# Expert up product with the weights as the stationary operand, in a one-core Trainium2 kernel

## The reference

```python
def expert_block(args):
    tok, wgt, e = args
    xb = h[tok]
    hid = jax.nn.silu(xb @ exp_gate[e]) * (xb @ exp_up[e])
    return (hid @ exp_down[e]) * wgt[:, None]
```

## Time and profile before

| | |
|---|---|
| median of 3 runs | 2751.93 us (2748.4 to 2758.2) |
| profiled execution: time | 2754.09 us |
| profiled execution: span | 2751.3 us |
| TensorE busy | 2628.2 us, 96% of the span |
| VectorE busy | 1655.5 us, 60% |
| ScalarE busy | 726.8 us, 26% |
| granted TensorE clock, mean over the span | 0.978 of full speed |
| moved by DMA | 347.50 MB |

### The profile page before, as it was taken

The page is one execution under the profiler, slowest core; times in us unless marked ns, Lnnn a source line. Parts: engine busy times, 40 slices in busy tenths (PEclk is TensorE's granted clock), DMA queues, the critical chain, the costliest instruction groups (busy, mean ns, idle before and its releaser), DMA issues. The chain is left out here.

```text
span 2751.3 us, 54243 instructions
## 1 busy us (share of the span) xinstructions
PE 2628.2 (96%) x21528; PEld 1725.3 (63%) x21528; DVE 1655.5 (60%) x4435; ACT 726.8 (26%) x1772; POOL 310.8 (11%) x415
## 2 busy tenths in 40 slices
PE   6999989999999999999999999999999898899996
PEld 4888856664588744688544467777777655444443
DVE  5444267786555657665556368888888667322225
ACT  3211056651310000000000246555666300100002
POOL 0000033310000000000000000111110100634312
PEclk9999999999999999999999999999999999899998
DMA  6010035331022346223445411100000030799995
GB/s 247 32 62 31 1 138 170 124 110 45 30 78 92 138 168 214 68 86 110 152 170 180 157 63 29 29 3 29 29 21 11 18 126 31 291 397 401 399 365 206
DMA packets 108845, 347.50 MB, mean 126 GB/s; under 512 B 8752, under 2 KB 18480, under 8 KB 99520
## 3 DMA queue, kind: packets, MB, share of 16 engines
q1 hardware_dynamic: 100160, 319.00, 31.9%
q0 software_dynamic: 8448, 25.18, 2.5%
HBM read 311.05 MB, written 33.10 MB: 125 GB/s over the span
## 5 line engine op out<-in xcount | busy, mean ns | idle before, releaser
L2076 PE MATMUL mixing_ps<-all_main,pre_ws 64*64 64x256 f32 x3072 | 245.9, 380 | 0.0
L3096 PE MATMUL ex_ps<-all_main,ex_xT 128*128 128x512 f32 x512 | 231.9, 596 | 12.1 <-DVE ex_xT L3250 10.2
L1318 PE MATMUL mlp_ps<-mlp_w2s,all_main 128*128 128x512 f32 x512 | 239.6, 592 | 0.0
L1318 PE MATMUL mlp_ps<-all_main 128*128 128x512 f32 x384 | 183.2, 592 | 0.7 <-DVE all_main L1541 0.7
L3096 PEld LDWEIGHTS ex_ps<-all_main,ex_xT 128*128 128x128 f32 x512 | 95.2, 191 | 121.4 <-issue 117.6
L1318 PEld LDWEIGHTS mlp_ps<-mlp_w2s,all_main 128*128 128x128 f32 x512 | 96.6, 190 | 117.8 <-issue 105.1
L2076 PEld LDWEIGHTS mixing_ps<-all_main,pre_ws 64*64 64x64 f32 x3072 | 126.5, 134 | 27.2 <-issue 4.0
L254 PE MATMUL qkv_ps<-qkv_wq,h_hT 128*128 128x256 f32 x576 | 134.0, 385 | 2.9 <-DVE h_hT L547 2.9
L1318 PEld LDWEIGHTS mlp_ps<-all_main 128*128 128x128 f32 x384 | 72.7, 190 | 93.2 <-issue 70.2
L254 PEld LDWEIGHTS qkv_ps<-qkv_wq,h_hT 128*128 128x128 f32 x576 | 111.1, 193 | 19.7 <-issue 4.1
L1532 DVE TENSOR_TENSOR all_main<-mlp_w2s 128x512 f32<-128x512 f32 x64 | 44.2, 690 | 131.1 <-PE mlp_ps L1318 129.5
(11 more groups left out here) (486 smaller groups left out, 5041.6 us busy)
## 6 DMA issues: line engine op xcount, KB each, us to landing
mlp_w2s<-in_w SPq DMA_DIRECT2D x64, 1024.0 KB, 5.0
all_main<-in_w_gu SPq DMA_DIRECT2D x32, 2048.0 KB, 14.8
all_early<-in_w SPq DMA_DIRECT2D x32, 1024.0 KB, 4.8
att_wa<-in_w_ada SPq DMA_DIRECT2D x32, 512.0 KB, 3.9
all_early<-in_w_d SPq DMA_DIRECT2D x16, 1024.0 KB, 17.4
all_main<-in_w_d SPq DMA_DIRECT2D x16, 1024.0 KB, 17.4
y_rows<-ex_y SPq DMA_DIRECT2D x32, 512.0 KB, 9.8
qkv_wq<-in_w_qkv SPq DMA_DIRECT2D x6, 2048.0 KB, 7.5
```

What stands on the lines that cost most here:

```text
L1318: last = nc.tensor.matmul(ps[:, PRODUCTS.index(name), :], lhsT=lhsT, rhs=rhs, start=j == 0, stop=j == FPAIRS - 1)
L2076: last = nc.tensor.matmul(ps[heads(m), banks[half], 0:UT], lhsT=ws[heads(half), n, k, heads(m)], rhs=columns(k, heads(half)), start=(k == ...
L3096: last = nc.tensor.matmul(pg[:, n % 2, :], lhsT=xT[:, n % 2, k * P:(k + 1) * P], rhs=gu[n][:, k, :], start=(k == 0), stop=(k == KT - 1))
```

## The change

In the up product the operands change places. Blocks of 128 columns of `gu` (cell c of 4, slice k of 8) are stationary and the 128 gathered rows of `xT` stream. The result in `pg` has hidden features on partitions and rows along the free axis: columns 0 to 255 hold the two gate blocks, 256 to 511 the two up blocks. Silu and the multiply keep their shapes, and `hid` comes out as `hT` was. The turns, the copy to `hT`, the accumulators `ph`, the tile `hT` and the semaphores `h_turned` and `h_taken` go. The up product is 32 matmuls in place of 8, split 20 and 12 where it was 5 and 3. With no turn between them, the two parts follow one another. The waits for reuse of `hid` are now on `downed`.

```diff
-                def up(ring, b, n, ks):
-                    for k in ks:
-                        last = nc.tensor.matmul(pg[:, n % 2, :], lhsT=xT[:, n % 2, k * P:(k + 1) * P], rhs=gu[n][:, k, :], start=(k == 0),
-                                                stop=(k == KT - 1))
-                    if ks[-1] == KT - 1:
+                def up(ring, b, n, cells):
+                    for cell in cells:
+                        c, k = cell // KT, cell % KT
+                        last = nc.tensor.matmul(pg[:, n % 2, c * P:(c + 1) * P], lhsT=gu[n][:, k, c * P:(c + 1) * P],
+                                                rhs=xT[:, n % 2, k * P:(k + 1) * P], start=(k == 0), stop=(k == KT - 1))
+                    if cells[-1] == CELLS - 1:
                         last.then_inc(ring.gated, 1)
-
-                def turn_h(ring, b, n):
-                    for j in range(2):
-                        last = nc.tensor.transpose(ph[:, n % 2, j * P:(j + 1) * P], hid[:, n % 2, j * P:(j + 1) * P], ident[:])
-                    last.then_inc(ring.h_turned, 1)
 
                 def down(ring, b, n):
                     for half in range(2):
                         for j in range(2):
-                            last = nc.tensor.matmul(py[:, half, :], lhsT=hT[:, n % 2, j, :],
+                            last = nc.tensor.matmul(py[:, half, :], lhsT=hid[:, n % 2, j * P:(j + 1) * P],
                                                     rhs=dn[n][:, j, half * NB:(half + 1) * NB], start=(j == 0), stop=(j == 1))
                     last.then_inc(ring.downed, 1)
 
-                FIRST, REST = range(0, 5), range(5, KT)
+                CELLS = 4 * KT
+                FIRST, REST = range(0, 20), range(20, CELLS)
...
-                def p_turn_h(b, n):
+                def p_down(b, n):
                     pe.wait_ge(pipe.hidden, b + 3)
-                    pe.wait_ge(pipe.h_taken, b + 1)
-                    turn_h(pipe, b, n)
-
-                def p_down(b, n):
-                    pe.wait_ge(pipe.h_taken, b + 3)
                     pe.wait_ge(pipe.y_taken_a, b + 1)
                     pe.wait_ge(pipe.y_taken_v, b + 1)
                     down(pipe, b, n)
...
                         p_up_first(b + 1, (n + 1) % NW, j + 1 + (n + 1) // NW)
-                        p_turn_h(b, n)
                         up(pipe, b + 1, (n + 1) % NW, REST)
                         p_down(b, n)
...
                 def p_hidden(b, n):
                     dve.wait_ge(pipe.silu, b + 1)
-                    dve.wait_ge(pipe.h_turned, b + 1)
+                    dve.wait_ge(pipe.downed, b + 1)
                     hidden(pipe, b, n)
-
-                def p_take_h(b, n):
-                    dve.wait_ge(pipe.h_turned, b + 3)
-                    dve.wait_ge(pipe.downed, b + 1)
-                    take_h(pipe, b, n)
...
                         p_turn_x(b + 2, (n + 2) % NW, j + 1 + (n + 2) // NW)
-                        p_take_h(b, n)
                         p_hidden(b + 1, n + 1)
                         p_take_y(b, n, 2 * j + n // 2 + 1)
```

More of the change, by code:

```diff
@@ L2949, in stage_experts_combine @@
         hid = s.sb("hid", [P, 2, D_EXP])
-        hT = s.sb("hT", [P, 2, 2, P])
         y = s.sb("y", [P, 2, D])
@@ L2963, in stage_experts_combine @@
         ps = s.ps("ps", [P, 2 * RING, NB])
-        plist, pg, ph, py = (ps[:, 2 * n:2 * n + 2, :] for n in range(4))
-        names = "x_turned gated silu hidden h_turned h_taken downed y_taken_a y_taken_v"
+        plist, pg, py = (ps[:, 2 * n:2 * n + 2, :] for n in (0, 1, 3))
+        names = "x_turned gated silu hidden downed y_taken_a y_taken_v"
         class Ring:
@@ L2971, in stage_experts_combine @@
         for ring, tag in ((pipe, "p"), (more, "o")):
-            (ring.x_turned, ring.gated, ring.silu, ring.hidden, ring.h_turned, ring.h_taken, ring.downed,
+            (ring.x_turned, ring.gated, ring.silu, ring.hidden, ring.downed,
              ring.y_taken_a, ring.y_taken_v) = (s.sem(f"{tag}_{n}") for n in names.split())
@@ L3143, in _ @@
                 pe.sem_inc(pipe.gated, 2)
-                pe.sem_inc(pipe.h_turned, 2)
                 pe.sem_inc(pipe.downed, 2)
@@ L3158, in _ @@
                         p_up_first(b + 1, (b + 1) % NW, EXPERTS // NW)
-                    p_turn_h(b, b % NW)
                     if b + 1 < EXPERTS:
@@ L3180, in _ @@
                         pe.wait_ge(more.x_turned, b + 2)
-                        up(more, b, 0, range(KT))
+                        up(more, b, 0, range(CELLS))
                         pe.wait_ge(more.hidden, b + 1)
-                        turn_h(more, b, 0)
-                        pe.wait_ge(more.h_taken, b + 1)
                         down(more, b, 0)
@@ L3260, in hidden @@
                                             ).then_inc(ring.hidden, 1)
-                def take_h(ring, b, n):
-                    nc.vector.tensor_copy(hT[:, n % 2, :, :].rearrange("p a b -> p (a b)"), ph[:, n % 2, 0:2 * P]
-                                          ).then_inc(ring.h_taken, 1)
                 def take_y(ring, b, n):
@@ L3355, in _ @@
                 nc.vector.memset(eps[:], LN_EPS).then_inc(scaled, 1)
-                dve.sem_inc(pipe.h_taken, 2)
                 dve.sem_inc(pipe.y_taken_v, 1)
@@ L3371, in _ @@
                         p_turn_x(b + 2, (b + 2) % NW, EXPERTS // NW)
-                    p_take_h(b, b)
                     if b + 1 < EXPERTS:
@@ L3389, in _ @@
                         hidden(more, b, 0)
-                        dve.wait_ge(more.h_turned, b + 1)
-                        take_h(more, b, 0)
                         dve.wait_ge(more.downed, b + 2)
```

## The result

The changed kernel takes 2763.37 us (median of 9 runs, 2760.11 to 2766.67), the kernel before 2752.47 (9 runs beside them, 2747.12 to 2758.2). The ratio is 1.004 with a 95% interval of 1.003 to 1.0051: 10.9 us or 0.4% slower. The profiled execution of after has a time of 2763.37 us and a span of 2761.6, against 2751.3 before, so there are 10.3 us of span to find.

A forecast was written before the change was run, and what follows sets the result against it. TensorE, busy 96% of the span, was taken as the bound, with DMA full beside it at 400 GB/s. +1.4 - 0.3 = +1.1 us on the 2751.9 median gave 2753.0 us; own range 2749 to 2758, whole range 2745 to 2775.

The forecast's parts named there:

- The pitch: Up product: each of 64 records, a 128x128 load with 128 moving columns, takes 0.1117 us, so 7.15 us a block.
- the period: Steady expert block: 7.15 us up plus 3.43 us down is 10.58 us, +0.06 us a block.
- the 24 later blocks: Blocks 8 to 31, from 2441.43 us to the end: +0.06 us each, +1.4 us together.
- the last block: Before down(31): without turns it waits only for y's copy, so it starts 0.33 us sooner and most of 1.28 stays.
- the rate: DMA in the expert stage: a little under the earlier 400 GB/s, at 396.
- the weights' earlier landing: Gate and up weights in the expert stage: time from issue to landing falls below 14.3 us.
- slower: Whole kernel more than 0.3% (8.3 us) slower: chance 0.20.
- part 2: Turns and copy: hidden copy gains nothing; the first seven blocks' 0.4 us disappears in TensorE's 5.5 us of weight waits.
- Rival A: Every up record: weight loads don't hide; +28 us at a pitch of 0.125, +220 us with nothing hidden; chance 0.11.
- Rival C: Expert stage: DMA bounds at a 10.46 us period, waits for w_d appear, -1.7 us, 2750 us; chance 0.10.
- Rival B: TensorE's loop: larger code is fetched again at six jumps back, 10 to 31 us, 2763 to 2784 us; chance 0.15.
- the forecast's mechanism: Whole kernel: +1.4 us over the later blocks and -0.3 us before the last down product, +1.1 us.

The follow-up runs named there:

- after_spread: Changed kernel with all gathers kept but their series broken up by GpSimd's comparisons and, in the loop, a wait on an earlier up product: 2750.53 us, 0.9995 of before.
- before_split: Kernel before, operands and turns kept, with each 512 moving columns of the up product in four matmuls of 128: 2766.58 us, 1.0055.
- 1: Changed kernel run again unedited, 2764.63 us, ratio 1.0048; and without the expert stage's weight loads for blocks 2 to 31, 2763.61 us.
- 2: TensorE's loop written out, so it never jumps back: in the changed kernel 2765.12 us (1.004), in the kernel before 2751.27 us (0.9998).
- 6: Changed kernel with 80 semaphore increments ahead of TensorE's first up product, shifting its later instructions: 2765.35 us.
- 4: All gathers kept but their series broken up: in the changed kernel 2750.53 us (0.9995), in the kernel before 2748.87 us (0.9994).
- 8: Changed kernel with only the first gather series broken up, plus 12 more tiny indirect DMAs a loop pass: 2890.65 us.
- 3: Changed kernel with the gathers of blocks 2 to 31 left out, a semaphore raised in their place: 2747.08 us.
- 5: Changed kernel with only the first gather series broken up, 2761.18 us (1.0035), or only the loop's later gathers made to wait, 2759.26 us (1.0021).
- after_no_loads: Changed kernel without the expert stage's weight loads for blocks 2 to 31, which compute on whatever the buffers hold: 2763.61 us.

## Why the prediction was right in its range and wrong in its cause

**Right, and by its own steps.** The pitch (0.1117), the period (10.58), the 24 later blocks (+1.42 for +1.4), the last block (-0.27 for -0.33), the rate (397 GB/s for 396) and the weights' earlier landing (13.1 on the page, where before's page has 14.8) came out as worked out. At the last block y's copy is the next late thing, as the step said:

```profile
2701.82 3.60 PE L3104 MATMUL ex_ps<-all_main,ex_hid 128*128 128x512 f32 x8
2705.45 0.69 DVE L3249 COPY ex_y<-ex_ps 128x512 f32<-128x512 f32 x1 [2.60 <-PE ex_ps L3104]
2706.29 3.67 PE L3104 MATMUL ex_ps<-all_main,ex_hid 128*128 128x512 f32 x8 [0.88 <-DVE ex_y L3249]
```

By the prediction's own line of 0.3% for what can't be told from no change, the measured 0.4% (0.3 to 0.51) is slower, a case to which it gave 0.20.

**The step that failed** is the sentence in part 2 that the first seven blocks are covered, their 0.4 us disappearing in the waits for weights. It priced them at nothing; they cost +11.1 us. The 5.5 us of the earlier trace rows were also misread, for they add up TensorE's products and its weight loads, which waited side by side at the same two places (us, times, longest; from the waits of before):

```profile
PEld ex_ps L3096 <- DMA all_main<-in_w_d: 3.6, 2, 2.2
PE ex_ps L3096 <- DMA all_main<-in_w_d: 1.9, 2, 1.3
```

By its blocks, before loses 0.24 + 1.59 + 0.87 = 2.7 us there. That was still cover enough: in `after_spread`, which has the change and no gaps, down(6) ends 82.4 us after the first up record, 2.1 sooner than before. What the step didn't see is that the up product now needs 128 array instructions in 7.15 us where it needed 32 in 6.9, and that TensorE's supply of them is held up twice in just these blocks. Against `after_spread`, after loses 27.8 - 18.9 = 8.9 us up to down(0) and 95.6 - 82.4 - 8.9 = 4.3 us from there to down(6). Less the 2.1 that `after_spread` is ahead of before, that gives the +11.1. Of the 8.9, some 2.5 are the clock at half behind the first stretch. Some 1.2 more belong to the start: the clock stays at 0.50 for the first 5.6 us of records in after and for 3.2 in `after_spread`, before any gap, and nothing in the runs ties that to the gaps. The other 5.2 are the gaps themselves.

**Why before shows nothing of it** is known in part. `before_split` shows that short records alone bring the gaps. The earlier trace rows showed that TensorE's queue holds some 12 records, which is 12 x 0.43 = 5.2 us of work with 512 columns and 1.3 us with 128; the first stretch in after is 5.5 us long, with two records inside it. But before's own second series has 28 issues, from 2378.3 to 2417.3, beside three blocks of 10.52 us and one of 10.76, and 5.2 us of work can't bridge the 20 us of it that lie beyond the point where after has gaps. The rate fits better there: in the milder stretch of after 3 to 5 records come every 1.45 us, 2.1 to 3.4 per us, and before needs 1/0.43 = 2.3. Both are argued from these numbers, not shown.

**Rival A** (loads that don't hide) is refuted by the pitch of 0.1117, which every block behind the gaps keeps. By the Trainium skill's rule of 81 ns for a load and its matmul at 128 columns (TensorE: Matmul & The Clock Gate, Back-to-back issue gap), scaled as in the prediction, it would be an estimated 0.159; the measurement decides against that for f32. **Rival C** (DMA the bound) would show waits for w_d and a period of 10.46; there are none, and it is 10.58.

**Rival B** (the loop's code fetched again) named the right place in the machine, TensorE's supply of instructions, and its range of 2763 to 2784 us even holds the result, but it isn't what happened. The packets in two stretches of after (packets, MB, share of the 16 engines; in the second, 2420 to 2680 us, the view has no line of instructions at all):

```profile
q8 instruction: 3, 0.05, 0.3%
```

```profile
q1 hardware_dynamic: 34620, 91.26, 91.7%
q0 software_dynamic: 4272, 11.67, 11.9%
```

A body of 576 array instructions is run seven times from code fetched once, and no jump back costs anything. With the Trainium skill's 128 KiB for TensorE (Runtime: NRT & Kernel Launch, Instruction fetch mechanics) the trace agrees; a forced fetch at each jump outside a window of two pages it doesn't show. The time fell in this rival's range by chance, and outside the forecast's own range of 2749 to 2758.

**What stays open** is how GpSimd's issues hold up TensorE. The runs exclude full DMA engines (1), new code (2), a place in the code (6), GpSimd's work in general (4) and a late fetch of code (8), and tie it to unbroken series of indirect DMAs (3, 4, 5, 8). Whether it is their issue or their descriptors, and which path the two engines share, no run tells apart.

**The best version** is the change with the gathers spread, about 0.9995 / 1.004, so 0.45% faster than the changed kernel (worked out from two ratios to before, not compared directly). It can't be told from the kernel before. The fairest comparison has the gathers spread in both: 2750.53 with the change and 2748.87 without, 1.7 us apart where the forecast's mechanism gives 1.1, and within the scatter of both. The change itself brings no gain even when nothing disturbs it: TensorE saves the turns and spends 0.06 us a block more in all.

## What to carry to other kernels

Count the instructions that an engine needs per microsecond, and not only its busy time: a product cut into four times as many short ones costs almost nothing in steady state (0.06 us of 10.58 here), but it shows a held-up supply of instructions that the long ones didn't show. "issue" gaps on one engine can come from what a neighbour does, so lay the other engines' timelines beside them, and break up long rows of gather issues with work that has to be done anyway. Where the steady state is known to a hundredth of a microsecond, price the start of the stage by itself. And add up waits from one lane of an engine only.

## What the runs showed of the hardware that was not expected

- Unbroken series of GpSimd's indirect DMA issues (1.25 us each) hold back TensorE's instructions. The gaps begin 11 to 20 us into the series. Behind most series they go on for 1.1 to 2.9 us (4.7 behind the one of 48); beside two series of 20 they were over by its end, in `after_no_loads` 5.0 us sooner. Single f32 records then come 0.7 to 2.8 us apart, and no packet of instructions is under way. Two series of 16 cost 12.8 us by the medians of `after` and `after_spread`; one of 48 and five of 20 cost 140 us.
- In the 4.9 us behind the first such stretch of after the granted clock was 0.50, and in the stretch itself 0.83 on the mean.
- A 128x128 f32 load with 128 moving columns is sustained at 0.1117 us a record, whichever operand is held; a steady period of 10.58 us with 72 loads is kept for 24 blocks at a clock of 1.00.
